# Gate products between the score matmuls and the turns of an attention stage: chunks cut in two halves

## The reference, cut to what matters

```python
proj = h @ lw['w_in']                      # h: 640 x 1024
...                                        # split: conv parts, q/kv latents, g_conv, g_mla (1024 columns)
s = (jnp.einsum('bqhd,bkhd->bhqk', qn_b, k_nope)
     + jnp.einsum('bqhr,bkr->bhqk', qr_b, k_rope)) * ATTN_SCALE
p = jax.nn.softmax(s.astype(jnp.float32), axis=-1).astype(v.dtype)
o = jnp.einsum('bhqk,bkhd->bqhd', p, v)
y_mla = o @ lw['w_o']
merged = jax.nn.sigmoid(g_conv) * y_conv + jax.nn.sigmoid(g_mla) * y_mla
```

## Time and profile before

| | |
|---|---|
| time, median of 3 runs | 943.6 us (942.42 to 944.73) |
| time of the profiled execution | 942.75 us |
| its span | 940.5 us |
| TensorE's matmuls busy | 877.8 us, 93% of the span |
| weight loads, VectorE, ScalarE, GpSimd busy | 695.0, 416.1, 277.3, 111.2 us |
| mean granted TensorE clock | 0.981 of full |
| attention stage | from 107 to about 264 us |

### The profile page before, as it was taken

How to read it: one execution, slowest core, us unless ns; L and a number is a source line. 1 busy time by engine, 2 the same in 40 slices (tenths; PEclk the granted TensorE clock), 3 DMA queues, 4 the chain that set the end, 5 groups by cost and what they waited for, 6 DMA issues and landing times. The chain is left out here.

```text
span 940.5 us, 15004 instructions
## 1 busy us (share of the span) xinstructions
PE 877.8 (93%) x6016; PEld 695.0 (74%) x6016; DVE 416.1 (44%) x892; ACT 277.3 (29%) x522; POOL 111.2 (12%) x123
## 2 busy tenths in 40 slices
PE   3798988989999999999999999995899999999997
PEld 3587666777899999999999998884555555555552
DVE  1358345445534343351521266538534344343433
ACT  5336654445620311212121232333111111111122
POOL 0000000000000000000000021021232333323330
PEclk9899999999999999999999999997799999999999
DMA  9945443622213212212223222779999999999948
GB/s 330 352 175 187 153 188 110 192 66 68 66 53 90 76 59 89 88 46 89 68 71 130 68 90 73 240 255 352 383 412 416 415 414 416 413 416 414 415 184 334
DMA packets 73679, 198.83 MB, mean 211 GB/s; under 512 B 11384, under 2 KB 43112, under 8 KB 61080
## 3 DMA queue, kind: packets, MB, share of 16 engines
q1 hardware_dynamic: 65800, 181.71, 51.9%
q0 software_dynamic: 7824, 16.36, 4.6%
HBM read 189.30 MB, written 18.17 MB: 221 GB/s over the span
## 5 line engine op out<-in xcount | busy, mean ns | idle before, releaser
L810 PE MATMUL pair<-w_ug,xgT 128*64 128x256 f32 x1184 | 138.3, 387 | 1.2 <-ACT xgT L947 1.2
L1904 DVE TENSOR_TENSOR lo<-raw,hi 128x2048 fp32r<-128x2048 f32 (+3 forms) x32 | 69.4, 2168 | 114.0 <-ACT hi L1721 113.2
L1721 ACT CAST hi<-raw 128x2048 fp32r<-128x2048 f32 (+3 forms) x31 | 53.8, 1734 | 218.1 <-PE pair L1345 202.1
L1343 PE MATMUL pair<-hT,hi 128*128 128x320 f32 x512 | 116.7, 309 | 0.0
L1345 PE MATMUL pair<-hT,lo 128*128 128x320 f32 x512 | 116.7, 309 | 0.0
L1341 PE MATMUL pair<-hT,hi 128*128 128x320 f32 x512 | 116.6, 309 | 0.0
L810 PEld LDWEIGHTS pair<-w_ug,xgT 128*64 128x64 f32 x1184 | 84.8, 139 | 42.0 <-issue 4.5
L1341 PEld LDWEIGHTS pair<-hT,hi 128*128 128x128 f32 x512 | 85.6, 188 | 0.2 <-issue 0.2
L1345 PEld LDWEIGHTS pair<-hT,lo 128*128 128x128 f32 x512 | 85.7, 188 | 0.0
L1343 PEld LDWEIGHTS pair<-hT,hi 128*128 128x128 f32 x512 | 85.5, 188 | 0.0
L829 PE MATMUL pair<-w_dn,actT 128*64 128x512 f32 x296 | 71.7, 605 | 1.3 <-issue 1.3
(11 more groups left out here) (350 smaller groups left out, 1467.4 us busy)
## 6 DMA issues: line engine op xcount, KB each, us to landing
w_ug<-in_w_up SPq DMA_DIRECT2D x32, 1024.0 KB, 21.6
w_ug<-in_w_gate SPq DMA_DIRECT2D x32, 1024.0 KB, 24.3
w_dn<-in_w_down SPq DMA_DIRECT2D x32, 1024.0 KB, 21.2
raw<-in_w_in SPq DMA_DIRECT2D x20, 1024.0 KB, 5.3
ada_a<-in_w_ada SPq DMA_DIRECT2D x14, 1024.0 KB, 11.3
raw<-in_w_ada SPq DMA_DIRECT2D x10, 1024.0 KB, 6.3
ya<-expert_rows SPq DMA_DIRECT2D x5, 1024.0 KB, 9.1
raw<-in_w_conv_out SPq DMA_DIRECT2D x4, 1024.0 KB, 5.0
```

The lines of the kernel that those rows point to most:

```text
L810: x = pe.matmul(bank[2 + d % 2][g * SL:(g + 1) * SL, 0:DE], xgT[d % 2][:, k, h * SL:(h + 1) * SL], w_ug[r][:, g, h, k, :], start=(n == 0), ...
L1343: pe.matmul(o, st[0], m[1], start=False, stop=False)
L1721: act.copy(hi[n % 2][:, 0:size], raw[n % 4][:, 0:size]).then_inc(hi_done, 1)
L1904: dve.tensor_sub(lo[n % 2][:, 0:size], raw[n % 4][:, 0:size], hi[n % 2][:, 0:size].bitcast(F32)).then_inc(lo_done, 1)
```

## The change

Each chunk of 8 k-steps is cut into two halves of 4 k-steps (12 matmuls). `room` lists the units that take a half: -1 (ahead of unit 0) and every unit up to 38 but 0, 4, 9, 14 and 5, 15, 25, 35. Half j % 2 of chunk j // 2 stands in the j-th of them. A half stands behind `scores(n + 2)` and ahead of the value products, the modulation products and the turn. The waits of a chunk stand ahead of its first half, its semaphore behind its second. `gm_out` follows in ScalarE's pass of the same unit, behind `exps(n + 1)` and ahead of the wait for the turn. The splits of pieces 6 and 8 start at units 16 and 31 in place of 17 and 32.

```diff
-    gm_turn = {n: g for g, n in enumerate((-1, 2, 5, 7, 10, 12, 16, 19, 22, 24, 26, 29, 31, 33, 36, 38))}
+    room = [n for n in range(-1, len(units) - 1) if n not in ada_turn and n not in (5, 15, 25, 35)]
+    gm_turn = {n: (j // 2, j % 2) for j, n in enumerate(room)}
+    assert len(room) == 2 * N_CHUNK
     split_turn = {}
-    for n, first in ((N_GM + 1, 5), (N_GM + 2, 17), (N_GM + 3, 24), (N_GM + 4, 32)):
+    for n, first in ((N_GM + 1, 5), (N_GM + 2, 16), (N_GM + 3, 24), (N_GM + 4, 31)):
...
-        def gm_chunk(g):
+        def gm_chunk(g, half):
             n, (j, cs) = N_GM + g // 4, gm_block(g)
-            if g >= 1:
+            if half == 0 and g >= 1:
                 pe.wait_ge(gm_copied, g)
-            if g % 4 == 0:
+            if half == 0 and g % 4 == 0:
                 pe.wait_ge(lo_done, n + 1)
             wv = [v3(t, KD, 256) for t in (hi[n % 2], lo[n % 2])]
-            for k in range(KD):
+            for k in range(half * KD // 2, (half + 1) * KD // 2):
                 x = prod(bank[7][:, 0:HALF], [t[:, k, j % 2 * P:(j % 2 + 1) * P] for t in wv],
                          [hT(t, k)[:, cs] for t in range(2)], k == 0, k == KD - 1)
-            x.then_inc(piece_used if g % 4 == 3 else gm_done, 1)
+            if half:
+                x.then_inc(piece_used if g % 4 == 3 else gm_done, 1)
...
-        gm_chunk(gm_turn[-1])
+        gm_chunk(*gm_turn[-1])
         for n, (h, i) in enumerate(units):
             if n + 2 < len(units):
                 scores(n + 2)
+            if n in gm_turn:
+                gm_chunk(*gm_turn[n])
             if i == 0 and h >= 1:
                 pv(h - 1)
             if n in ada_turn:
                 ada_att(n)
             p_turn(n)
-            if n in gm_turn:
-                gm_chunk(gm_turn[n])
...
-            if n - 1 in gm_turn:
-                gm_out(gm_turn[n - 1])
+            if n in gm_turn and gm_turn[n][1]:
+                gm_out(gm_turn[n][0])
             act.wait_ge(s_tp, n + 1)
```

## The result

The changed kernel takes 930.8 us, median of 4 runs (929.85 to 931.8), against 944.2 of the kernel before on the same chip: a ratio of 0.9851, 95% interval 0.9831 to 0.9872.

A forecast was written before the change was run, and what follows sets the result against it. Attention was taken as bound by TensorE's order of work, with the gain in its gaps. Waits -8.8, clock -1.7 and switches +2.2 gave -8.3 us: 934.5 from the profiled 942.75, 935.3 for the median, 80% range 932.2 to 940.0.

The forecast's parts named there:

- Term 2, the waits: TensorE in attention: six waits for probabilities (7.2 us) and one for the exp (1.6) go, -8.8 us.
- the margin of 0.08: ScalarE's chain of 4.01 us against 4.09 us of TensorE's new work, covered by just 0.08, at units 5 and 25.
- Term 1, the switches: TensorE entering gate matmuls: 32 x 0.10 = 3.2 us after, 1.0 before, so +2.2 us.
- the lower bound: Switches on TensorE might cost nothing at all: -1.0 us in place of +2.2.
- Term 3, the clock: The clock's fall behind unit 12's 2.31 us wait is saved, -1.7 us.
- Rival (a): The clock falls once elsewhere, in attention or at the router: price 1.7 us, 937.0 us, chance 0.15.
- The moved splits: Third gate piece's load, its split now at unit 16, not 17: hidden, with at least 2 us spare.
- The 0.9 us wait: Wait for ScalarE's copy at unit 38's turn moves to unit 39's turn, at the same price.
- (b): Waits come back in smaller pieces, 0.13 us at each of 31 units, 4.0 us: 939.3 us, chance 0.13.
- (c): Gain isn't carried to the end, expert stage paced by its loads; or halves change nothing: 943 us, chance 0.08.
- (d): Switches between gate matmuls and transposes stall TensorE; decides from 0.36 us per half; at 0.45, 946.5 us; chance 0.06.

The follow-up runs named there:

- two_moved: Kernel of before with only the whole chunks of units 7 and 12 moved ahead of their turns, with their copies out of bank 7: 940.2 us, ratio 0.9948.
- splits_late: Changed kernel with the two moved weight splits back at units 17 and 32: 935.8 us, ratio 0.9902 to the kernel before.
- whole_ahead: Kernel of before with whole chunks of 24 matmuls, in their 16 places, between scores and turn, copy out of bank 7 in same unit's pass: 943.9 us, ratio 0.9985.

## Why the prediction was wrong, by its own steps

The direction, the mechanism and the carry to the end were right. Two terms of the sum were mis-sized: the waits, taken at the idle time shown, and the switches, priced at rows behind a wait. The sum was 8.3 us against 12.9 in attention. To take the waits at their full price I set the start of one block against the start of the next. Rows of the kernel before that weren't shown:

```profile
118.72 0.71 PE L1528 MATMUL pair<-cst,prob 128*128 128x128 f32 x5
119.37 0.49 PE L1514 MATMUL pair<-kT,qT 96*128 96x128 f32 x2
120.64 0.77 PE L1528 MATMUL pair<-cst,prob 128*128 128x128 f32 x5 [0.79 <-DVE prob L2076]
...
185.52 0.71 PE L1528 MATMUL pair<-cst,prob 128*128 128x128 f32 x5
186.27 1.34 PE L1511 MATMUL pair<-kT,qT 96*128 96x320 f32 x4
187.79 0.33 PE L1528 MATMUL pair<-cst,prob 128*128 128x128 f32 x1 [0.17 <-DVE prob L2076]
...
196.84 0.71 PE L1528 MATMUL pair<-cst,prob 128*128 128x128 f32 x5
199.17 0.49 PE L1514 MATMUL pair<-kT,qT 96*128 96x128 f32 x2 [1.62 <-ACT prob L1807]
200.69 0.76 PE L1528 MATMUL pair<-cst,prob 128*128 128x128 f32 x5 [1.03 <-DVE prob L2076]
...
223.50 1.24 PE L1511 MATMUL pair<-kT,qT 96*128 96x320 f32 x4
224.82 0.33 PE L1528 MATMUL pair<-cst,prob 128*128 128x128 f32 x1
```

**Term 2, the waits: 8.8 forecast, 10.8 measured.** The 0.79 us wait stands between blocks whose starts are 1.27 us apart, where two prompt matmuls without a wait take 0.22 (118.97 to 119.19 above): it cost 1.05. So 1.62 is 1.79, 1.03 is 1.30, 2.65 is 2.83, 2.31 is 2.47, 0.17 is 0.44 and 0.21 is 0.37: 10.25 for 8.78 shown. And three delays aren't shown as waits of a matmul at all: 0.65 and 0.75 where a turn takes 0.54, and scores at 223.50 with their turn at 224.82, 1.32 where 1.08 is the rule: 0.56 more. That they are waits, and for the same two engines, the weight loads at these three places tell:

```profile
119.37 0.30 PEld L1514 LDWEIGHTS pair<-kT,qT 96*128 96x128 f32 x2 [0.18 <-ACT prob L1807]
...
186.27 0.84 PEld L1511 LDWEIGHTS pair<-kT,qT 96*128 96x128 f32 x4 [0.27 <-ACT prob L1807]
...
224.81 0.14 PEld L1528 LDWEIGHTS pair<-cst,prob 128*128 128x128 f32 x1 [0.58 <-DVE prob L2076]
```

A matmul is shown for longer than it holds the engine (0.31 us for a gate matmul, whose row advances by 0.147), and that much of a wait lies under it. The step that took the shown idle time as the price was mis-sized by 2.0 us; two_moved bears out the measure. The chains that I set against TensorE's work were right: no wait appeared where cover was said to be, not even at the margin of 0.08.

**Term 1, the switches: +2.2 forecast, -0.2 left over**, that is, what remains of 12.91 after 10.81 for the waits, 1.7 for the clock and 0.19 for the last value products (0.85 to 0.66 from the last turn to them). This is the larger miss, and a mistake of reading. Both rows that I took the price from stood behind a wait: the eight scores of the earlier trace rows behind 0.73 us, the turn of the earlier trace rows behind 2.65. The group behind a wait is longer: 0.77 or 0.76 for 0.71 us in a turn, 0.49 for 0.39 in a pair of prompt scores, and 2.42 in those eight scores, where four show 1.24 and four more add 1.08. These 0.10 and 0.06 are what I charged to the switches, the 0.10 for all 32 halves. (A turn behind value products is 0.77 long without a wait too, in both kernels.) Where there is neither, the first gate matmul takes 0.15 behind scores and behind turns, and 44 added switches cost 0.02 each at most. The 0.2 left over needs no switch either: the price of a wait above ends where the turn starts, and in the kernel before four turns and three single transposes behind a wait, each with a gate chunk right behind it, hold TensorE 0.05 to 0.06 longer than others, some 0.4 us in all. The runs show the switches at nothing, though not at the gain of 1.0 that I had as the lower bound, since the switches of before were free too. The sentence on weight loads pulled ahead, which I took from the Trainium skill ("TensorE: Matmul & The Clock Gate", Step-by-step: what each phase is for) and held against the row of 0.25 us, was the better guide here. The changed kernel's trace agrees: the weight load of the gate matmul behind the scores of 117.61 starts at 118.43, before the 1.08 us of those scores are over at 118.69.

**Term 3, the clock: -1.7 forecast, -1.7 between the two profiles, 1.5 more against the second profile of before.** In six profiles of kernels with a wait of 2.3 us or more, or with the waits at unit 22, the clock fell in attention, each time behind such a wait and once or twice; in five with no wait over 0.9 us it didn't. Nearly the forecast's price, then, but at more than one place. Rival (a) happened in the form of a fall ahead of attention, at 57 us, in six of eleven profiles, kernels of both sorts, so it belongs to no change. Another fall, behind a wait of 2.04 us at 563 to 579 us, came in four of eleven, and the change's two profiles both have it. The 12.9 us of the profiles and the 13.4 of the medians need no reconciling: the interval of the ratio is 12.1 to 16.0 us. How often executions without a profile lost once or twice in attention isn't known, as they show a mean clock alone.

**The moved splits.** I had them as hidden and asked only if the load would be in time. It was. That the early split was needed, for unit 21's half, I didn't ask; splits_late puts 4.9 us on it.

**The 0.9 us wait** moved from unit 38's turn to unit 39's at the same price, as said. **The rivals:** (b) small waits, none appeared in attention; (c) nothing was lost on the way to the end; (d) switches, 0.02 us against the 0.36 from which it decides.

**The range.** Its lower end, 932.2, was built from switches at nothing alone. The waits had no bound of their own below, though the trace had start times for one; with 2.0 us for them it would have reached 930.2 and held the time.

## What to carry to other kernels

Price a wait from the start of the block ahead of it to the start of the one behind it, less what the pair takes where nothing waits: the idle time shown was short by 0.16 to 0.27 us each, and a few delays of 0.1 to 0.24 showed only in the weight loads' rows, 2 us on 8.8 together. Take the price of a switch, or of any single instruction, from a place that isn't behind a wait, and not from one place alone. Where two engines in series answer TensorE, filler in one lump covers one chain and bares the other; cut so that nearly every unit (31 of 40 here) has a piece between the scores and the turn, and look what the earlier reader of a buffer now needs sooner: neither the halves behind the turn, nor whole chunks ahead of it, nor the halves without the earlier splits gave more than two thirds.

## What the hardware showed that I had not expected

The granted clock fell to half, for 3.4 us each time, behind a wait of 2.3 us in each of three profiles that have it behind unit 12's scores, and never behind the 2.65 us wait of the same three, 22 us earlier; behind the pair of 1.6 and 1.0 us at unit 22 it fell in two of three, and in whole_ahead behind the 1.6 us alone. Outside attention every profile has a wait of 1.94 us at 56 us and one of 2.04 us behind attention; the clock fell behind the first in six of eleven and behind the second in four. A fall loses 1.7 us by the shares of the clock, and 1.5 us of attention between the two profiles of before. So a short wait can cost its own length again; which one does isn't seen from its length, and the same wait can do it in one execution and not in the next.
